# A two-block transformer on one core: weights first on two queues, x split during the tile before, and the gates' root spread inside a tile

## The reference

```
# first block, h is 272 x 1024
for layer in range(2):
    u = rmsnorm(h, mix_norm[layer])
    if layer == 0:                      # w_in: hq hf hi hg cq ckv kr
        mix = concat(hgrn2_mixer(...), mla_mixer(...)) @ w_out
    else:
        mix = multiscale_pool(u, pool_w, pool_scale)
    h = h + mix
    h = h + relu(rmsnorm(h, mlp_norm[layer]) @ w_up[layer]) ** 2 @ w_down[layer]
# second block, x = h[16:], 256 x 1024
for i in range(2):
    h = rms_norm(x, g_pre_mix[i])
    mix = short_conv_mixer(h, ...) if i == 0 else diff_attention(h, ...)
    x = x + rms_norm(mix, g_post_mix[i])
    x = x + rms_norm(conv_ffn(rms_norm(x, g_pre_ffn[i]), ...), g_post_ffn[i])
    gate = sigmoid(rms_norm(x, g_pre_ple[i]) @ w_gate)          # "gate" below
    x = x + rms_norm(gate * (p[i] @ w_proj), g_post_ple[i])     # p[i] @ w_proj is "embed" below
```

## Time and profile before

| What | Before |
|---|---|
| Median of three runs | 1285.33 us (1282.17 to 1288.28) |
| The profiled execution, its own time | 1285.41 us |
| Its span, first to last instruction | 1283.5 us |
| TensorE (PE) busy | 1243.3 us, 97%, 10153 instructions |
| VectorE (DVE) busy | 909.2 us, 71% |
| ScalarE (ACT) busy | 739.3 us, 58% |
| Granted TensorE clock, mean | 0.988 |
| DMA | 205.51 MB, mean 160 GB/s |

### The profile page before, as it was taken

The page is one execution under the profiler, slowest core; times in us unless marked ns, Lnnn a source line. Parts: engine busy times, 40 slices in busy tenths (PEclk is TensorE's granted clock), DMA queues, the critical chain, the costliest instruction groups (busy, mean ns, idle before and its releaser), DMA issues.

```text
span 1283.5 us, 24399 instructions
## 1 busy us (share of the span) xinstructions
PE 1243.3 (97%) x10153; PEld 1218.3 (95%) x10153; DVE 909.2 (71%) x1577; ACT 739.3 (58%) x1262; POOL 6.4 (0%) x16
## 2 busy tenths in 40 slices
PE   4999999999999999999999999999999999999997
PEld 4989889999999999999999999999899899999997
DVE  5895656765456776445686899965787768999656
ACT  6854345664445666334556666564766866665644
POOL 1000000000000000000000000000000000000000
PEclk9998999999999999999999999999899999999998
DMA  6222323755553555554564566664355335666630
GB/s 248 88 89 82 99 82 129 233 177 185 168 163 115 185 192 183 191 184 157 164 214 132 179 195 194 189 209 161 102 185 177 116 115 167 197 196 189 206 131 33
DMA packets 58889, 205.51 MB, mean 160 GB/s; under 512 B 6515, under 2 KB 8860, under 8 KB 58524
## 3 DMA queue, kind: packets, MB, share of 16 engines
q1 hardware_dynamic: 57104, 201.77, 48.6%
q10 hardware_dynamic: 1676, 2.19, 0.5%
HBM read 202.87 MB, written 1.06 MB: 159 GB/s over the span
## 4 chain that ended last, share of the span: by engine, by line
PE 87%; DVE 6%; ACT 5%; DMA 1%; issue 1%; ACTq 0%; DVEq 0%
PE PS L367 69%; PE PS L409 6%; PE PS L378 2%; DVE WL L352 1%; ACT WH L345 1%; PE PS L398 1%; PE PS L516 1%; PE PS L458 1%; DMA RAW<-wpack 1%; PE PS L2335 1%; ACT EE L2493 1%; PE PS L658 1%; ACT L528 0%; PE PS L689 0%; PE PS L2402 0%
## 5 line engine op out<-in xcount | busy, mean ns | idle before, releaser
L352 DVE TENSOR_TENSOR WL<-RAW,WH 128x1024 fp32r<-128x1024 f32 (+2 forms) x385 | 460.3, 1201 | 206.5 <-ACT WH L345 206.0
L345 ACT ACTIVATE WH<-RAW 128x1024 fp32r<-128x1024 f32 (+2 forms) x385 | 391.9, 1038 | 216.0 <-PE PS L367 185.4
L367 PE MATMUL PS<-UH,WH 128*128 128x256 f32 (+2 forms) x1576 | 448.5, 285 | 4.5 <-DVE WL L352 2.7
L367 PE MATMUL PS<-UH,WL 128*128 128x256 f32 (+2 forms) x1576 | 447.6, 284 | 0.0
L367 PE MATMUL PS<-UL,WH 128*128 128x256 f32 (+2 forms) x1576 | 447.2, 284 | 0.0
L367 PEld LDWEIGHTS PS<-UH,WH 128*128 128x128 f32 (+1 forms) x1576 | 298.1, 189 | 5.5 <-DVE WL L352 3.0
L367 PEld LDWEIGHTS PS<-UH,WL 128*128 128x128 f32 (+1 forms) x1576 | 298.4, 189 | 0.0
L367 PEld LDWEIGHTS PS<-UL,WH 128*128 128x128 f32 (+1 forms) x1576 | 296.7, 188 | 0.0
L367 PE MATMUL PS<-HL,WH 128*128 128x272 f32 (+1 forms) x512 | 145.7, 285 | 0.0
L367 PE MATMUL PS<-HH,WH 128*128 128x272 f32 (+1 forms) x512 | 145.6, 284 | 0.0
L367 PE MATMUL PS<-HH,WL 128*128 128x272 f32 (+1 forms) x512 | 145.4, 284 | 0.0
(11 more groups left out here) (395 smaller groups left out, 1916.9 us busy)
## 6 DMA issues: line engine op xcount, KB each, us to landing
RAW<-wpack SPq DMA_DIRECT2D x363, 512.0 KB, 4.2
RAW<-wpack SPq DMA_DIRECT2D x16, 384.0 KB, 3.6
RAW<-wpack SPq DMA_DIRECT2D x6, 256.0 KB, 2.9
X<-xin SPq DMA_DIRECT2D x1, 1088.0 KB, 5.0
C<-cst SPq DMA_DIRECT2D x1, 1072.0 KB, 10.1
HB<-bias_rows ACTq DMA_DIRECT2D x1, 1024.0 KB, 5.8
out<-X SPq DMA_DIRECT2D x4, 256.0 KB, 2.4
VF<-cst ACTq DMA_DIRECT2D x1, 512.0 KB, 3.8
```

Of the source, the lines that this page charges most:

```text
L345: a.e.activation(WH[n % NH][:, 0:w], RAW[n % NR][:, 0:w], ACT.Copy).then_inc(*a.mark("wh", n))
L352: v.e.tensor_tensor(WL[n % NH][:, 0:w], RAW[n % NR][:, 0:w], WH[n % NH][:, 0:w].bitcast(f32), ALU.subtract).then_inc(*v.mark("wl", n))
L367: ins = t.e.matmul(o, part(n, hw, kw, a, b), x(kx), start=first and not i and not p, stop=last and i == len(kcs) - 1 and p == 2)
```

## The change

The change has these parts.

- Start, loading: SP now issues weight unit 0, x's parts 2 and 3, unit 1, x's parts 6 and 7, the identity, unit 2, the gains of all later norms, unit 3. ACT issues the first eight gains and x's other four parts on its own queue. The constants `C` come behind two more weight units.
- Start, order: TensorE runs 24 fillers, then the first tile of hf with one filler between parts and six behind, then the second tile, then the sums of the squares, and the spread of the root stands in the middle of the third tile. ACT brings the table of the square root first, makes weight unit 0, splits x, and only then squares it; units 2 and 3 stand before the root, and the later ones behind the copy of the spread. DVE makes the low part of unit 0 and x's low parts before it adds squares.
- First MLP: parts 0 to 3 of x are split in the mixer's last tile, into two new buffers `U2H` and `U2L`, as `UH` and `UL` are still read there. The 18 fillers go.
- Convolution: the low parts of six parts of x are made as the second MLP's last tile runs. The 24 fillers go. ACT's DMA of `PI` moves behind six parts.
- ffn and gate: of embed's eight tiles, five stay at the entry to ffn, and three move to the entry to gate, the sixth ahead of the spread of ffn's root, two behind it, with two fillers in place of 18. `w_ple_proj` is loaded in three units for this, the last ahead of gate's weights.
- Gate: the spread of gate's root stands after four of the eight parts of the third pair's first tile. ACT brings the sigmoid's table before it copies the spread, and the weight units among the sigmoids and squares stand elsewhere.

```diff
-        for c in (0, 512):
-            u.append(("ple", "w_ple_proj_2", layer, [0, 1], cols(c, c + 512)))
+        for c, z in ((0, 512), (512, 640)):
+            u.append(("ple", "w_ple_proj_2", layer, [0, 1], cols(c, z)))
...
+        u.append(("ple", "w_ple_proj_2", layer, [0, 1], cols(640, 1024)))
...
-            s.e.dma_start(X[:, :, :], xin).then_inc(*s.mark_dma("x"))
-            s.e.dma_start(G[:, :], gains).then_inc(*s.mark_dma("g"))
+            load_unit(s, 0)
+            s.e.dma_start(X[:, 2:4, :], xin[:, 2:4, :]).then_inc(*s.mark_dma("xp1"))
+            load_unit(s, 1)
+            s.e.dma_start(X[:, 6:8, :], xin[:, 6:8, :]).then_inc(*s.mark_dma("xp3"))
             s.e.dma_start(ID[:, :], cst[:, CAT["id"]:CAT["id"] + 128]).then_inc(*s.mark_dma("id"))
-            for n in range(NR):
-                load_unit(s, n)
+            load_unit(s, 2)
+            s.e.dma_start(G[:, 8:NG], gains[:, 8:NG]).then_inc(*s.mark_dma("g"))
+            load_unit(s, 3)
...
+            def first_tile():
+                b = banks.take(t, ("hf", 0), ("ev", "hf", 0))
+                for k in range(8):
+                    ins = products(t, PS[:, b, 0:T], unit_at["hf", 0], [(k, k)], 0, 128, xh_full, xl_full, u_ready, k == 0,
+                                   k == 7)
+                    if k < 7:
+                        keep_going(t, 1, done=("ones",))
+                ins.then_inc(*t.mark("mix", "hf", 0))
+                sig.also(("used", unit_at["hf", 0]), ("mix", "hf", 0))
+                keep_going(t, 6, done=("ones",))
...
+                products(t, PS[:, b, 0:T], n, pairs[0:4], 0, 128, xh_full, xl_full, u_ready, True, False)
+                root_spread(t, "m", T)
+                products(t, PS[:, b, 0:T], n, pairs[4:8], 0, 128, xh_full, xl_full, u_ready, False, True).then_inc(
...
+            t.wait_ge("ones", 0)
+            keep_going(t, 24)
+            first_tile()
+            project("hf", (1,), "ev")
             root_sum(t, "m", 0, T, ("rk", "m"))
-            root_spread(t, "m", T)
-            project("hf", range(4), "ev")
+            tile_with_root()
+            project("hf", (3,), "ev")
...
-            a.wait_ge("g")
-            a.wait_ge("ones", 2)
-            a.wait_ge("x")
+            a.e.dma_start(G[:, 0:8], gains[:, 0:8]).then_inc(*a.mark_dma("gm"))
+            for p in (0, 2):
+                a.e.dma_start(X[:, 2 * p:2 * p + 2, :], xin[:, 2 * p:2 * p + 2, :]).then_inc(*a.mark_dma(f"xp{p}"))
+            preload(a, ACT.Sqrt)
+            act_split(a, 1)
+            a.wait_ge("gm")
+            for j in range(8):
+                a.wait_ge(f"xp{j // 2}")
+                split_hi(a, ("m", j), UH[:, j, :], X[:, j, :], g("mix0", j))
+                if j == 5:
+                    act_split(a, 2)
             for p in range(4):
                 square(a, "m", 0, p, X[:, 2 * p:2 * p + 2, :], T)
-            for j in range(8):
-                split_hi(a, ("m", j), UH[:, j, :], X[:, j, :], g("mix0", j))
+            act_split(a, 4)
+            a.wait_ge("ones", 2)
             root_sqrt(a, "m", T)
             root_keep(a, "m", 0, T)
-            act_split(a, 4)
+            a.wait_ge("g")
...
-            v.wait_ge("g")
-            v.wait_ge("x")
+            dve_split(v, 1)
+            v.wait_ge("gm")
+            for j in range(8):
+                v.wait_ge(f"xp{j // 2}")
+                split_lo(v, ("m", j), UL[:, j, :], X[:, j, :], g("mix0", j), UH[:, j, :])
+            dve_split(v, 2)
             for p in range(4):
                 add_squares(v, "m", 0, p, T)
-            for j in range(8):
-                split_lo(v, ("m", j), UL[:, j, :], X[:, j, :], g("mix0", j), UH[:, j, :])
+            dve_split(v, 4)
             root_recip(v, "m", T)
+            v.wait_ge("g")
             lbg = G[:, GAT["lb"]:GAT["lb"] + 4]
             v.e.tensor_tensor(LO, lbg, lbg, ALU.subtract).then_inc(*v.mark("lb", 0))
-            dve_split(v, 4)
...
+                if j == 7:
+                    low_parts(v, 0, range(4))
...
+                U2H, U2L = (sb(n, [128, 4, T], f32r, scope=sc) for n in ("U2H", "U2L"))
...
+            h, l = (U2H, U2L) if layer == 0 and j < 4 else (UH, UL)
...
-            if layer == 0:
-                keep_going(t, 18)
...
-            end_mlp(a, layer)
             for p in range(4):
+                if p == (0 if layer else 2):
+                    end_mlp(a, layer)
...
-                for j in (2 * p, 2 * p + 1):
-                    split_lo(v, (st, j), UL[:, j, 0:w], X_(j, tok0), g(f"mlp{layer}", j), UH[:, j, 0:w])
+                if layer or p > 1:
+                    low_parts(v, layer, (2 * p, 2 * p + 1))
...
+                        if (layer, gg, k0, m) == (1, 3, 24, 1):
+                            conv_parts(v, range(6))
...
-            p.wait_ge("mix", "wout", 7)
-            p.wait_ge("res", "m", 7)
+            p.wait_ge("up", 0, 31)
...
-            keep_going(t, 24)
...
+                if p == 3:
+                    a.wait_ge("down", 1, 3, 24, 1)
+                    a.wait_ge("res", "mlp1", 7)
+                    a.e.dma_start(PI[:, :, :], pin[0]).then_inc(*a.mark_dma("pin", 0))
...
+            conv_parts(v, (6, 7))
...
+                    x, j_, last = (0, 0, 3) if j < 4 else (1, 4, 4) if j < 5 else (2, 5, 7)
+                    n, at = unit_at["ple", 3 * layer + x], 128 * (j - j_)
...
-            embed(2, 8)
+            embed(2, 5)
...
+            embed(5, 6)
             root_spread(t, f"f{layer}", S)
-            keep_going(t, 18, f"f{layer}")
+            embed(6, 8)
+            keep_going(t, 2, f"f{layer}")
...
-                        products(t, PS[:, b, 0:S], n + m, pairs, 0, 128, uh, ul, g_ready).then_inc(
-                            *t.mark("gate", layer, u, m))
+                        products(t, PS[:, b, 0:S], n + m, pairs[0:4], 0, 128, uh, ul, g_ready, True, False)
                         if (u, m) == (2, 0):
                             root_spread(t, st, S)
+                        products(t, PS[:, b, 0:S], n + m, pairs[4:8], 0, 128, uh, ul, g_ready, False, True).then_inc(
...
-            enter_scalar(a, st, prev, f"gpf{layer}", lambda p: embed(*((1, 3), (3, 5), (5, 7), (7, 8))[p]))
+            enter_scalar(a, st, prev, f"gpf{layer}", lambda p: embed(*((1, 2), (2, 4), (4, 5), (5, 5))[p]))
...
-            enter_scalar(a, st, prev, f"gpp{layer}", lambda p: None)
+            enter_scalar(a, st, prev, f"gpp{layer}", lambda p: embed(*((5, 5), (5, 7), (7, 8), (8, 8))[p]))
...
+            preload(a, ACT.Sigmoid)
+            root_keep(a, st, 0, S)
             act_split(a, n0 + NH + 1)
-            root_keep(a, st, 0, S)
-            preload(a, ACT.Sigmoid)
...
-            act_split(a, n0 + 2 + NH)
             gate_sigmoid(0)
             gate_sigmoid(1)
+            act_split(a, n0 + 3 + NH)
+            gate_square(0)
+            gate_square(1)
             act_split(a, n0 + 4 + NH)
-            gate_square(0)
             embed_gain(a, layer, 0)
-            gate_square(1)
             act_split(a, n0 + 5 + NH)
...
-            dve_split(v, n0 + 2 + NH)
             product_gate(0)
+            dve_split(v, n0 + 1 + NH)
             product_gate(1)
             dve_split(v, n0 + 3 + NH)
...
-            s.e.dma_start(C[:, :], cst[:, 128:NCA]).then_inc(*s.mark_dma("c"))
             for n in range(NR, NU):
                 load_unit(s, n)
+                if n == NR + 1:
+                    s.e.dma_start(C[:, :], cst[:, 128:NCA]).then_inc(*s.mark_dma("c"))
```

36 lines of the change are left out of this document (22 added, 14 removed).

## The result

The changed kernel takes 1272.4 us (median of 6 runs, 1266.68 to 1276.58) against 1284.0 (6 runs beside them): a ratio of 0.9899, 95% interval 0.987 to 0.9928, or 9 to 17 us less, 13.0 in the middle. Predicted were 13.8 us less and 1271.6 us. The profiled execution takes 1274.14 us with a span of 1272.2, 11.3 less than before's 1283.5.

A forecast was written before the change was run, and what follows sets the result against it. TensorE makes up 87% of the chain, so only its time without useful products can be won; in the mixer DVE sets the gain. Terms 5.0 + 2.0 + 2.6 + 2.0 - 0.2 + 2.3 + 0.1 = 13.8; 1285.4 - 13.8 = 1271.6 us, range 1266 to 1278.

The forecast's parts named there:

- the sign that I named: Mixer: prediction is wrong if the stretch from K's first step to the mixer's end changes by more than 2 us.
- A: Start and mixer: new loading and order gain 5.0 us, between 2.9 and 6.2; K's first step near 33 us.
- 3.3 us: Start, lower end: half clock for 7 us of the first tiles, 30 products costing 0.11 us more each.
- B: First MLP: 18 fillers go and four parts of x are made early; gain 2.0 us (1.5 to 2.2).
- C: Convolution: 24 fillers go and six parts are made in the last tile; gain 2.6 us (2.0 to 2.9).
- D: Two entries to ffn: three embed tiles leave each; gain 1.0 us each, 2.0 together (0.6 to 3.4).
- E: Two entries to gate: three tiles and two fillers replace 18 fillers; -0.1 us each, -0.2 together (-1.0 to 0).
- F: First gate's end: earlier spread and table load bring sigmoids about 2.7 us earlier; gain 2.3 us (0 to 2.8).
- (1): Rival: the start gives little, 2.0 us, as holes bring the half clock; 1274.6 us, chance 0.24.
- (2): Rival: DVE doesn't bind, its order has slack; the start gains 9.5 us; 1267.1 us, chance 0.11.
- (3): Rival: the early parts aren't early, so B and C give nothing; 1276.2 us, chance 0.09.
- (4): Rival: slower, as holes without fillers cost the clock 5 us each, 20 us for four; 1291.6 us, chance 0.04.

The follow-up runs named there:

- swapped banks: Changed kernel with the sixth and seventh product tile swapping PSUM banks at both ffn; 1269.6 us, ratio 0.9872; repeated on another chip 1270.5 us, 0.9889.
- one queue: Changed kernel with the first gains and all parts of x issued by SP, none by ACT; 1268.54 us in one execution.
- late table: Changed kernel with the sigmoid's table at the gates loaded behind the copy of the root's spread, as before; 1270.49 us in one execution.
- no fillers at the start: Changed kernel without the 24 fillers that TensorE runs before its first product; 1271.4 us in one execution.
- embed as before: Changed kernel with eight embed tiles at ffn's entry, 18 fillers at gate's and w_ple_proj in two units, as before; 1271.49 us, ratio 0.9895.
- early scan: Changed kernel plus swapped banks; weight units 4 and 5 split before the copy of the root's spread, 8 to 11 later; 1272.31 us, ratio 0.9887.
- run without fillers: Kernel before without the 18 fillers ahead of the first MLP and the 24 ahead of the convolution; 1287.95 us, ratio 1.0007.
- squares first: Early scan kernel with unit 10 split before the scan, plus ACT squaring the attention output's last two tiles before weight units; 1264.49 us, ratio 0.9825.
- start alone: Kernel before with only the new start (loading, first hf tiles, ACT's and DVE's order up to the root); 1278.37 us, ratio 0.9936.

## Why the prediction was right or wrong

**What bounds: right up to the heads; the check of it was in part luck.** K's first step came at 32.72 (33.0 predicted), and the stretch from there to the end of the mixer has 158.75 us after 158.42. But DVE sets the pace only as far as the product behind the heads, 43.3 us from the scan (43.5 before). From there to the mixer's end TensorE is busy for 102.57 of 104.70 us, and the granted clock decides. The changed kernel:

```profile
86.70:191.40 104.70, 102.57 (x726) 90.59 (x727) 63.04 (x114) 45.59 (x82) 0.00 (x0) 0.95 0.30 96
```

and with the two banks swapped, the same program up to the end of the mixer:

```profile
87.00:188.60 101.60, 99.43 (x726) 88.89 (x726) 63.12 (x114) 45.66 (x82) 0.00 (x0) 0.98 0.31 100
```

| runs | K's first step, us | half level behind the heads, us | K to mixer's end, us |
|---|---|---|---|
| swapped banks, one queue, late table | 33.11, 34.77, 33.83 | 3.4 each | 155.58 to 155.60 |
| swapped banks, repeat | 32.76 | 6.8 | 157.22 |
| changed, its repeat, no fillers at the start | 32.72, 32.88, 33.76 | 10.2 each | 158.75 to 158.78 |
| embed as before | 32.61 | 20.5 | 163.55 |

At the same clock a shift of K passes through to 0.03 us: that shows the mechanism better than the pair does. That the pair agreed to 0.3 is partly luck, as the two executions happen to have half levels of similar length there (13.7 us before, 10.2 after); the sign that I named, 2 us, would have failed in others by the clock alone.

**A: the mechanism right, a term mis-sized: 7.2 instead of 5.0.** The upper end, 6.2, assumed full clock and took 1.0 for ACT behind K; the full clock was there, the loss behind K was 0.6 (7.5 at K, 6.9 at LF + B), and K came 0.3 earlier than worked out. What failed is the lower end: "3.3 us" for a half clock of 7 us in the first tiles, and with it the 1.2 I took off between the ends. In the changed kernel's profile the hole of 1.72 us had no half level behind it. Where one came (without the fillers, with the late table, with the early scan) the spread was read 1.0 to 1.3 us later, not 3.3, and where the trace has a record of it, it lasted 3.4 us, not 7. That the spread was there at the predicted time is luck again: the first weight unit landed at 4.46 us and not at 5.5, so the queues did not share evenly, and the first product came 0.8 early; the first tile then took 4.8 us and not 3.8, as x's last part landed at 8.60 and TensorE waited 0.44 for its UL. All 1.1 MB were there by 5.85, as the row at 407 GB/s said.

**B and C: right**, 2.0 and 2.6 (in the repeat a hole of 0.48 is left at B), and for the reason given: with the early parts the products follow the last tile, and the run without fillers shows that taking fillers away alone gains nothing. What I did not see is the 1.5 between. The kernel before has this row, at 429.5 in the second MLP:

```profile
PE PS L367 <- DVE TB L1574: 1.0, 1, 1.0
```

It is the same collision as at ffn: the sixth tile wants the first tile's bank. The 18 fillers ahead of the first MLP take a bank, too; without them the tiles fall on other banks, and the wait is gone in the changed kernel and in the run without fillers alike (379.4 us for this stretch there).

**D: wrong**, -0.4 and -4.6 instead of 1.0 each. The step "the products start 2.0 us earlier and run at DVE's pace. Next is late: the weights behind them" holds as far as it goes: the wait for WL is 0.56 (0.7 predicted). But I stopped at the first late thing, and put the banks at nothing without counting them. Before, the sixth tile finds a bank that is free, and the first tile's goes to the seventh; now the sixth finds that of the first tile, which DVE can't read before the spread is there: 0.93 us, at each ffn. The swapped banks show it, and with them the two stretches have 98.57 and, without a half level, 121.05 and 121.11: 0.7 and 1.0 less than before, near what I took. What shifts the banks is embed's move at the first ffn; at the second the missing fillers do it alone, as the run without them and the run with embed as before have the wait there, too. At the second ffn a third thing is late: the weights land late, ACT is behind with the last squares, and TensorE waits 0.9 to 2.4 us for the sums in all nine profiles with the moved embed (the one with the squares first left out). In the four without it the wait is 0.25 (before), 0.75 (embed as before), 1.30 (no fillers) and under 0.15 (start alone), so embed's move is not the only cause. In four of the nine the half level follows. So the profiled -4.6 is a bad execution of that term; in the other one of the same kernel it is -0.4. Why the weights land later there, whether by the third, small unit of ple's weights, was not tried and stays open.

**E: right**, -0.1.

**F: right**, 3.0 instead of 2.3, a little above the upper end of 2.8. The wait is 0.2 (2.1 before), and the half level is 3.4 us shorter in this pair. The run with the start alone has the wait and the shorter half level, and 18.10 us against the 18.87 of before; so 2.3 is left at an equal half level, and 0.8 goes with the clock of before's execution. The table of Exp at the start took 1.28, and the next activation started 1.30 after its start: no drain is seen behind it, as in before's rows and unlike what the Trainium skill states (ScalarE: Activation LUTs, "What ACT_TABLE_LOAD costs").

**The rivals.** The start did not give little (1). DVE does bind up to the heads (2), though with the weights in their places the heads come 3.2 us earlier still, part of what rival 2 counted on. The early parts are early (3). Holes do cost the clock (4), but 1.6 us and not 5 each: I priced it from the one row at 0.50 for 10.2 us at the gate's end, a stretch that has holes in it and that lasted only 6.8 in other executions, with the wait there or not.

## What to carry to other kernels

A change in how many tiles are run ahead shifts every later tile to another bank, and so can taking away fillers, which take a bank in turn like a tile: count the banks through to the next root, in all later stages, before saying that only the weights are late. Taking fillers away gains only where the work they cover is moved as well, and then the hole has to go too, since it is paid for in the clock. Before a gain is read from one pair of profiles, compare how long each was at the half level. Where two engines are nearly balanced, a shorter chain on one pays only if the other's weights are not what was pushed behind, and on an engine that works in order, what others wait for goes ahead of what may land late.

## What the runs showed of the hardware

Holes of 1.86 and 2.10 us in TensorE's products were each followed by 3.4 us at the half level (the run without fillers). At the start, holes of 0.92 to 1.72 us ahead of the first product had none behind them in eight profiles, the changed kernel and its repeat among them; one of 1.77 with the sigmoid's table late, an edit 890 us later in the program, had one (8.62 to 12.04), and so had 2.49 with the early scan. With one queue a half level came at 9.51 though no hole was longer than 0.95. At the second ffn waits of 2.43, 2.41, 2.03 and 1.08 us were followed by one, and waits of 1.39, 1.30, 1.23, 1.08, 0.93 and 0.90 were not. So one profile doesn't tell how a kernel's clock will stand in the next execution: from the heads to the mixer's end the same program had 3.4 to 20.5 us at the half level, and by the table above 10.2 us of it cost 4.8. A stretch without a clock record shows PEclk 1.00 even where the products stand 0.23 apart; their spacing has to be read instead.
